# A section of the second layer's modulation is computed in the first layer's attention

## The reference

```python
for i in range(DEPTH):                       # DEPTH = 2
    mod = split(silu(c) @ w_mod[i] + b_mod[i], 6)        # sh1, sc1, ga1, sh2, sc2, ga2
    mod_c = split(silu(c_ctx) @ w_mod[i] + b_mod[i], 6)
    ...
def trunk_layer(x, xc, mod, mod_c, p, ang_row, ang_col, last):
    h = rmsnorm(x, g_pre_mix) * (1 + sc1) + sh1
    u = h @ w_in
    # four mixers: short convolution, latent attention (MLA), conformer convolution,
    # neighbourhood attention; concatenated into y
    x = x + ga1 * rmsnorm(y @ w_out, g_post_mix)
    hm = rmsnorm(x, g_pre_mlp) * (1 + sc2) + sh2
    x = x + ga2 * rmsnorm(square(relu(hm @ w_mlp1)) @ w_mlp2, g_post_mlp)
    # the same for the context xc, unless it is the last layer
```

## Time and profile before

| | |
|---|---|
| median of 3 runs | 1489.4 us |
| profiled execution, its own time | 1490.7 us |
| its span | 1488.8 us |
| TensorE busy | 1439.2 us (97%) |
| VectorE busy | 908.9 us (61%) |
| ScalarE busy | 671.6 us (45%) |
| DMA: 236.95 MB | 159 GB/s mean |
| second layer's attention, DMA, 770 to 792 us | 377 to 430 GB/s |

### The profile page before, as it was taken

How to read it: one execution, slowest core, us unless ns; L and a number is a source line. 1 busy time by engine, 2 the same in 40 slices (tenths; PEclk the granted TensorE clock), 3 DMA queues, 4 the chain that set the end, 5 groups by cost and what they waited for, 6 DMA issues and landing times.

```text
span 1488.8 us, 23403 instructions
## 1 busy us (share of the span) xinstructions
PE 1439.2 (97%) x9394; PEld 1231.1 (83%) x9394; DVE 908.9 (61%) x1388; ACT 671.6 (45%) x1060; POOL 38.0 (3%) x55
## 2 busy tenths in 40 slices
PE   5999998999999999999999999999999999999998
PEld 3787655888888888889856888998999999798996
DVE  3776555563241433579755665568998545796867
ACT  4421355562140413465155844455444564664544
POOL 0000000000000000000060000000000000000000
PEclk9999999999999999999999999999999999999999
DMA  9421675041331314236375555465445434455553
GB/s 394 160 85 57 236 290 211 4 159 65 114 112 59 132 35 144 82 126 218 114 269 212 198 189 178 147 221 184 170 170 170 165 133 145 142 195 192 176 198 114
DMA packets 33562, 236.95 MB, mean 159 GB/s; under 512 B 3712, under 2 KB 3840, under 8 KB 5696
## 3 DMA queue, kind: packets, MB, share of 16 engines
q1 hardware_dynamic: 32080, 228.31, 42.3%
q0 software_dynamic: 1392, 7.34, 1.5%
HBM read 234.58 MB, written 1.05 MB: 158 GB/s over the span
## 4 chain that ended last, share of the span: by engine, by line
PE 85%; DVE 5%; ACT 4%; DMA 4%; issue 1%; SPq 0%; DVEq 0%; ACTq 0%
PE ps L551 44%; PE ps L597 23%; PE ps L571 4%; DMA w<-in_stream 3%; PE ps L760 2%; PE ps L653 1%; PE ps L840 1%; PE ps L956 1%; DVE w_lo L436 1%; DMA U<-in_start 1%; PE ps L989 1%; PE ps L973 1%; ACT w_hi L426 1%; PE ps L961 1%; PE ps L689 1%
## 5 line engine op out<-in xcount | busy, mean ns | idle before, releaser
L551 PE MATMUL ps<-h_hi,w_hi 128*128 128x256 f32 (+1 forms) x1504 | 468.6, 312 | 3.7 <-DVE h_lo L2487 0.9
L551 PE MATMUL ps<-h_hi,w_lo 128*128 128x256 f32 (+1 forms) x1504 | 464.7, 309 | 0.0
L551 PE MATMUL ps<-h_lo,w_hi 128*128 128x256 f32 (+1 forms) x1504 | 464.6, 309 | 0.0
L426 ACT ACTIVATE w_hi<-w 128x1024 fp32r<-128x1024 f32 x332 | 333.2, 1053 | 246.3 <-DMA w<-in_stream 246.2
L436 DVE TENSOR_TENSOR w_lo<-w,w_hi 128x1024 fp32r<-128x1024 f32 x332 | 390.7, 1219 | 82.1 <-ACT w_hi L426 77.4
L551 PEld LDWEIGHTS ps<-h_hi,w_hi 128*128 128x128 f32 x1504 | 287.0, 191 | 20.6 <-issue 3.2
L551 PEld LDWEIGHTS ps<-h_lo,w_hi 128*128 128x128 f32 x1504 | 287.1, 191 | 15.0 <-issue 0.5
L551 PEld LDWEIGHTS ps<-h_hi,w_lo 128*128 128x128 f32 x1504 | 287.0, 191 | 14.5
L597 PE MATMUL ps<-w_hi,g_hi 128*128 128x512 f32 x472 | 185.0, 392 | 1.7 <-DVE g_lo L2340 0.9
L597 PE MATMUL ps<-w_lo,g_hi 128*128 128x512 f32 x472 | 183.8, 389 | 0.0
L597 PE MATMUL ps<-w_hi,g_lo 128*128 128x512 f32 x472 | 183.8, 389 | 0.0
(11 more groups left out here) (291 smaller groups left out, 1749.6 us busy)
## 6 DMA issues: line engine op xcount, KB each, us to landing
w<-in_stream SPq DMA_DIRECT2D x206, 1024.0 KB, 4.9
U<-in_start SPq DMA_DIRECT2D x4, 1024.0 KB, 11.4
w<-in_start SPq DMA_DIRECT2D x2, 1024.0 KB, 10.8
GA<-in_start SPq DMA_DIRECT2D x2, 1024.0 KB, 14.2
U<-in_bias POOLq DMA_DIRECT2D x2, 1024.0 KB, 6.0
SW<-in_small POOLq DMA_DIRECT2D x2, 896.0 KB, 5.0
X<-in_x SPq DMA_DIRECT2D x1, 1024.0 KB, 5.0
X<-in_ctx SPq DMA_DIRECT2D x1, 1024.0 KB, 7.2
```

Source lines behind the costliest of these rows:

```text
L426: act.activation(k.w_hi[:, c.slot, half], k.w[:, c.slot, half], ACT.Copy).then_inc(k.hi_done, 1)
L551: last = pe.matmul(k.banks(2 * c.pair, n, j * (512 if tiles == 2 else n)), w[a][:, c.slot, at:at + 128], h[b][:, kt * stride:kt * stride + n],
```

## The change

Section (1, 2) moves in the stream from the second layer's attention (`FILL_SECTIONS[1]`) to the first layer's. Its two rows steps and two features steps move from rows 0 and 1 of the second layer's table to rows 11 to 13 of the first layer's. Around them the other steps move: in the first layer rows(0, 0), rows(0, 1), gate(2, 3) and the gates of section 5 stand in other places, and in the second layer the steps of sections 3 to 5 come earlier and the two gate steps of section 2 stand in the attention, at place 0 of units 3 and 4, and no longer in the output product. The number of steps and of instructions is the same.

```diff
-FILL_SECTIONS = [[(0, 2), (0, 3), (0, 4), (0, 5), (1, 0), (1, 1)], [(1, 2), (1, 3), (1, 4), (1, 5)]]
+FILL_SECTIONS = [[(0, 2), (0, 3), (0, 4), (0, 5), (1, 0), (1, 1), (1, 2)], [(1, 3), (1, 4), (1, 5)]]
...
-                ([gate(2, 3)], [feats(5, 1)], [cf("cf_b", 1)]),
-                ([rows(0, 0, 1)], [rows(0, 1, 1)], [feats(0, 0, 1)]),
+                ([rows(0, 0, 1)], [feats(5, 1)], [cf("cf_b", 1)]),
+                ([rows(0, 1, 1)], [feats(0, 0, 1)], [gate(2, 3)]),
                 ([rows(1, 0, 1)], [feats(0, 1, 1)], [cf("cf_pw", 0)]),
                 ([rows(1, 1, 1)], [feats(1, 0, 1)], [cf("cf_pw", 1)]),
-                ([gate(5, 0)], [feats(1, 1, 1)], []),
-                ([gate(5, 1)], [], [gate(5, 2)]),
-                ([], [], [gate(5, 3)])]
-    return [([rows(2, 0)], [rows(2, 1)], [feats(2, 0)]),
-            ([cf("cf_t")], [rows(3, 0)], [feats(2, 1)]),
-            ([rows(3, 1)], [feats(3, 0)], [feats(3, 1)]),
-            ([rows(4, 0)], [rows(4, 1)], [feats(4, 0)]),
-            ([rows(5, 0)], [feats(4, 1)], [cf("cf_b")]),
+                ([rows(2, 0, 1)], [feats(1, 1, 1)], [rows(2, 1, 1)]),
+                ([gate(5, 0)], [feats(2, 0, 1)], [gate(5, 1)]),
+                ([feats(2, 1, 1)], [gate(5, 2)], [gate(5, 3)])]
+    return [([rows(3, 0)], [rows(3, 1)], []),
+            ([cf("cf_t")], [feats(3, 0)], [rows(4, 0)]),
+            ([], [feats(3, 1)], [rows(4, 1)]),
+            ([gate(2, 0)], [feats(4, 0)], [rows(5, 0)]),
+            ([gate(2, 1)], [feats(4, 1)], [cf("cf_b")]),
             ([rows(5, 1)], [cf("cf_pw")], [feats(5, 0)])]
...
-MOD_STEPS += [("features", DEPTH - 1, 5, 1), ("gate", DEPTH - 1, 2, 0), ("gate", DEPTH - 1, 2, 1)]
+MOD_STEPS += [("features", DEPTH - 1, 5, 1)]
...
-        for n, at in zip(OUT_STEPS, ((0, 0, 0), (0, 0, 5), (0, 1, 3))):
-            before[at] = lambda n=n: pe_mod_step(k, pe, n, 3)
+        before[0, 0, 0] = lambda: pe_mod_step(k, pe, LAST_COLUMNS, 3)
```

More of the change, by code:

```diff
@@ L102 @@
             MOD_STEPS += _steps
-OUT_STEPS = range(len(MOD_STEPS), len(MOD_STEPS) + 3)
-MOD_STEPS += [("features", DEPTH - 1, 5, 1), ("gate", DEPTH - 1, 2, 0), ("gate", DEPTH - 1, 2, 1)]
+LAST_COLUMNS = len(MOD_STEPS)
+MOD_STEPS += [("features", DEPTH - 1, 5, 1)]
 LAST_GATES = range(len(MOD_STEPS), len(MOD_STEPS) + 2)
@@ L1648, in act_mixers @@
     act_feed_rest(k, act, out)
-    if l == 1:
-        act_mod_step(k, act, OUT_STEPS[1], 3)
     transposed(end - 1)
-    if l == 1:
-        act_mod_step(k, act, OUT_STEPS[2], 3)
     outputs(end - 1)
@@ L2295, in dve_mixers @@
     if l == 1:
-        dve_mod_step(k, dve, OUT_STEPS[0], 3, o)
+        dve_mod_step(k, dve, LAST_COLUMNS, 3, o)
         feed_lo(k, dve, out + 1, (1,))
```

## The result

The changed kernel takes 1494.8 us (median of 22 runs, 1491.8 to 1500.6) against 1490.3 us for the kernel before in the same session (22 runs, 1488.3 to 1496.7): ratio 1.0025, 95% interval 1.0017 to 1.0033, which is +3.7 us (+2.5 to +4.9). Two further sessions gave 1.0022 (1.0013 to 1.0032) and 1.0016 (1.0004 to 1.0027). It is slower, by about what the forecast of +3.3 us said. As a time the forecast was 1492.7 us: the result is 2.1 us above it, 0.9 of which is that before itself came out at 1490.3 and not at the 1489.4 that the forecast starts from.

The account below looks back on a forecast made before the run. PE was taken as the bound, with 85% of the last-ending chain. First layer +7.6, second layer's attention -4.3, its output product -1.3 and clock +1.3 sum to +3.3 us, so 1492.7 us, range 1488.3 to 1495.8.

Parts of the forecast that it names:

- Work +4.9: First layer: two rows and two features steps come in on PE, 4.9 us, all on the path.
- waits gone: First layer: PE waits before transposes(14), values, the moved steps and features(0, 0) go, 3.3 us.
- gate(5, 1): First layer, unit 12: PE waits 1.9 us, since VectorE's features sum stands behind a low weight half awaiting ScalarE's high part.
- Cost 0: First layer: its stream takes 4 MB more, 10 us of transfer, without delaying PE.
- The rival with a stream that isn't relieved: Second layer still waits on DMA 1 to 2 us, total 1494 us; chance 0.18 shared by the two slower rivals.
- rows(4, 1): Second layer, unit 2: PE waits 2.8 us for VectorE's sum before the second rows step of section 4.
- 3.5 by items: Second layer's attention: 10.5 us going minus 7.0 coming makes a gain of 3.5 us.
- 4.4 step by step: Second layer's attention: following steps from scores(3) to the product gives a gain of 4.4 us; 4.3 was taken.
- 4 to 5 us less: Sign of being right: the second layer's stage lasts 4 to 5 us less.
- net -0.3: Second layer: a half-clock stretch worth 1.6 us goes, and one taken as 1.3 us comes behind the 2.8 us wait.
- The rival with a fall in the first layer: Clock also halves behind the first layer's waits, +1.3 us, 1494.5 us and more; chance 0.18 shared by the two slower rivals.
- The fast rival: First layer, at gate(5, 1): the high halves come earlier, hiding 4.8 us of waits, clock stays up, 1486.6 us; chance 0.08.

Follow-up runs that it names:

- experiment 1: Changed kernel with the first layer's middle feed of output weights moved behind place 1 on ScalarE and VectorE: 1490.7 us, ratio 0.9997 to the kernel before.
- experiment 2: As experiment 1, with the last weight chunks also fed one feed later: 1489.8 us, ratio 0.9994 to the kernel before.
- experiment 3: Changed kernel with second-layer rows(4, 0) and rows(4, 1) one place later, gate(2, 1) back in the output product: 1489.7 us, ratio 0.9992 to the kernel before.
- experiment 4: Second layer's part of the change alone, first layer as before, section (1, 2) left out: 1485.8 us, ratio 0.9973 to the kernel before.
- experiment 7: Changed kernel unedited, measured and profiled again: 1494.8 us, ratio 1.0022 to the kernel before.
- experiment 9: Changed kernel unedited, measured and profiled once more: 1494.6 us, ratio 1.0016 to the kernel before.

## Why the prediction was right

**First layer.** Work +4.9 and waits gone were as counted. New waits: before gate(5, 1) 1.81 (forecast 1.9), gate(5, 2) 1.81 (1.8), gate(5, 3) 0.92 in the two executions without a fall (1.1), gate(2, 3) 0.96 (0.9), small ones 0.25 (0.3). The stage came to +7.8 where the clock fell in it, and to +7.3 (51.1) where it stays. Experiments 1 and 2 took the causes away one after the other and got each wait back, so the mechanism is shown: a side step on PE stands behind a sum that stands behind a weight half. How much of it hangs on ScalarE's queue and how much on VectorE's isn't told apart, since both experiments moved the feed on both.

**Stream.** Cost 0 held: no wait on DMA in either layer, and the first output chunk held nobody. The rival with a stream that isn't relieved is out, by experiment 3 even with PE 5.8 us earlier.

**Second layer.** rows(4, 0) 1.33 (1.3), rows(4, 1) 2.45 (2.8), rows(5, 0) 0.29 (0.4), cf_b 0.29 (0.3). The term of 2.8 was too large by 0.35: in the queue of before that I took it from, the conformer norm's scalings last 1.29 us, and here they last 0.96; why isn't shown. My two sums for the stage disagreed, 3.5 by items and 4.4 step by step, and I took 4.3 without showing the second. Without a fall the stage lasts 46.2 us (experiments 1 and 4), 4.7 to 4.8 less than before, so the sum by items was the wrong one. With the fall it is 3.4 less. The "4 to 5 us less" among my signs left out the fall that my own sum had in this stage. The output product gave 1.4 (1.3), with the forecast wait for the low half, 0.26.

**Clock.** Forecast: one fall before, one after, in the same stage, net -0.3. Behind the 2.45 the clock did fall, in four traces (after, experiments 2, 7 and 9), and it didn't in two (experiments 1 and 4), with the same wait; stage 47.4 to 47.5 with, 46.2 without, so 1.3 us. Taking 1.3 as the term was right; that it had to be there at all was a matter of four traces to two. Runs of after have 6.2 to 7.9 us of half clock against 2.6 to 3.3 in before, and one fall in the traces of before and after is 3.2 to 3.4 us at half. That may be one fall a run more than I counted, but part of the difference can lie behind the last matmul, and of the three traces of after only the first has more falls (at 261 and 681 us). The rival with a fall in the first layer was worth +1.3 in my count; in the trace of after it cost 0.6. By the rule of the Trainium skill ("TensorE: Matmul & The Clock Gate", section "Why this matters for your kernels") none of these gaps was long enough; the traces disagree with it again, by the rows above.

**The number.** That the total came so close is in part luck. The forecast took the difference of one trace of before, with its one fall, and the stages of after's three traces make +3.1, +2.4 and +2.5 us. The sessions measured +3.7, +3.3 and +2.4, which scatter by as much as the clock term. And 1494.8 us lies above the forecast's own 1491.3 to 1494.2, where I had put the slower rivals; but the fall in the first layer is in only one of after's three traces, and the first output chunk didn't hold ScalarE.

**The fast rival.** It needed the low half 1.9 us earlier. The low half ended at 255.7, as worked out. Experiments 1 and 2 show that its place was the right one, by an edit, not by the change as it is.

## What to carry to other kernels

A step added on the engine that bounds costs its work and then what it waits for; write for each the queue of the engine that must read it first, and count from the starts, since four of six such sums came within 0.1 us. The same work, with the first layer's steps set ahead of a weight half and the second layer's rows steps one place later, turned +3.7 us into -6.0 us, so the order of the feed against the new step is to be changed with the table. Where a kernel is made to wait 2 us in several places, one trace doesn't tell how often the clock falls there: profile it more than once before a fall goes into a sum.

## What was not expected of the hardware

- The clock fell behind waits shorter than the 2.34 of the earlier trace rows: behind two of 1.81 within 5 us (granted 0.62 in the 2 us behind the second), but in only one of three executions of after. In experiment 3, with the same three waits, it fell behind the second, and the stretch at half was 6.8 us long (windows of 2 us from 262 us: 0.75, 0.50, 0.50, 0.54); it cost 1.8 us in the stage and about 1.0 behind it. At 681 us it fell in one execution of after, where PE had worked 0.94 us of the 2 us ahead and then waited 0.46 for a low half. Before and the two other executions of after have the same two waits there, 1.1 to 1.2 and 0.46 to 0.47 us, and no fall (windows, then timeline):

```profile
678.00:680.00 2.00, 0.94 (x8) 0.86 (x8) 1.74 (x4) 1.42 (x3) 0.08 (x1) 1.00 0.78 312
680.00:682.00 2.00, 1.54 (x10) 1.45 (x9) 1.97 (x4) 2.00 (x7) 0.00 (x0) 0.73 1.19 193
682.00:684.00 2.00, 2.00 (x11) 2.00 (x11) 1.90 (x7) 2.00 (x4) 0.00 (x0) 0.50 0.73 207
```

```profile
680.59 0.35 PE L551 MATMUL ps<-h_hi,w_hi 128*128 128x256 f32 x1 [0.46 <-DVE w_lo L436]
```

- A fall can be nearly free: in the first layer of after it lasted as long as in the second, but 0.6 us was all it cost (stage 51.67 against 51.09), as PE ran slowly in a time in which it would have waited 0.92 for ScalarE's copy.
